# Paged sample attention: keys by gathered four-page tiles and 32x32 transposes on VectorE, side projections moved beside the keys

## The reference, cut to what matters

```python
def dsa_sample(q, k, v, iq, iw, ik, cache_k, cache_v, cache_idx_k, page_table, rel_bias):
    ...
    idx, valid = dsa_select(iq, iw, ik_all, q_pos, topk)      # best 256 of 2056 keys per query
    k_sel = jnp.where(is_past, cache_k[phys, slot].astype(k.dtype), gather(k, nidx))
    v_sel = jnp.where(is_past, cache_v[phys, slot].astype(v.dtype), gather(v, nidx))
    return dsa_attend(q, k_sel, v_sel, idx, valid, q_pos, rel_bias)

def dsa_attend(q, k_sel, v_sel, idx, valid, q_pos, rel_bias):
    logits = jnp.einsum('bthd,btkhd->bthk', q, k_sel).astype(jnp.float32) * ATT_SCALE
    logits = logits + bias                                    # T5 relative bias
    p = jax.nn.softmax(jnp.where(valid, logits, -jnp.inf), axis=-1)
    return jnp.einsum('bthk,btkhd->bthd', p, v_sel)
```

## Time and profile before

| | us |
|---|---|
| Median of three runs | 1596.6 |
| Span of the profiled execution | 1593.2 |
| Key stretch, group 0 / group 1 | 115.7 / 104.6 |
| Softmax stretch, group 0 / group 1 | 15.4 / 17.3 |
| Value stretch, group 0 / group 1 | 110.8 / 101.3 |

### The profile page before, as it was taken

How to read it: one execution, slowest core, us unless ns; L and a number is a source line. 1 busy time by engine, 2 the same in 40 slices (tenths; PEclk the granted TensorE clock), 3 DMA queues, 4 the chain that set the end, 5 groups by cost and what they waited for, 6 DMA issues and landing times.

```text
span 1593.2 us, 32571 instructions
## 1 busy us (share of the span) xinstructions
PE 1471.7 (92%) x13518; PEld 1334.5 (84%) x13518; DVE 762.0 (48%) x1030; ACT 511.5 (32%) x818; POOL 234.5 (15%) x371
## 2 busy tenths in 40 slices
PE   7999998979979989899998998899799999999995
PEld 4867798957867778797777998799699999999995
DVE  5288699496514540025540135543555555552123
ACT  4243223324323341023341122122344455442121
POOL 3423234154210000000000000321000110000000
PEclk8899999989999999999999999899799999999998
DMA  5415223122159979999869976133322233223221
GB/s 173 149 27 159 65 80 113 57 96 73 49 188 369 332 249 342 383 358 329 310 223 402 363 258 240 34 125 104 113 80 80 80 90 95 83 98 102 79 83 60
DMA packets 179278, 266.58 MB, mean 167 GB/s; under 512 B 20522, under 2 KB 136539, under 8 KB 178043
## 3 DMA queue, kind: packets, MB, share of 16 engines
q1 hardware_dynamic: 167947, 243.95, 44.5%
q0 software_dynamic: 5104, 11.11, 2.1%
q10 hardware_dynamic: 6080, 9.44, 1.6%
HBM read 240.28 MB, written 24.18 MB: 166 GB/s over the span
## 4 chain that ended last, share of the span: by engine, by line
PE 77%; DVE 8%; DMA 5%; ACT 3%; SPq 2%; issue 2%; POOL 2%; ACTq 0%; DVEq 0%
PE PS L987 14%; PE PS L989 13%; PE PS L988 13%; PE PS L1197 8%; PE PS L1210 4%; PE PS L1245 3%; PE PS L1319 3%; PE PS L1318 3%; PE PS L1317 3%; DMA R<-in_cache_v 3%; PE PS L1028 2%; PE PS L1029 2%; PE PS L1030 2%; PE PS L1173 1%; PE PS L1120 1%
## 5 line engine op out<-in xcount | busy, mean ns | idle before, releaser
L987 PE MATMUL PS<-xn_hi,WH 128*128 128x288 f32 (+1 forms) x1424 | 430.7, 302 | 16.0 <-DVE xn_lo L1614 13.2
L988 PE MATMUL PS<-xn_lo,WH 128*128 128x288 f32 (+1 forms) x1424 | 424.7, 298 | 0.0
L989 PE MATMUL PS<-xn_hi,WL 128*128 128x288 f32 (+1 forms) x1424 | 424.6, 298 | 0.0
L987 PEld LDWEIGHTS PS<-xn_hi,WH 128*128 128x128 f32 (+1 forms) x1424 | 271.1, 190 | 33.1 <-issue 22.2
L988 PEld LDWEIGHTS PS<-xn_lo,WH 128*128 128x128 f32 (+1 forms) x1424 | 271.9, 191 | 0.0
L989 PEld LDWEIGHTS PS<-xn_hi,WL 128*128 128x128 f32 (+1 forms) x1424 | 271.6, 191 | 0.0
L582 DVE TENSOR_TENSOR WL<-W,WH 128x2048 fp32r<-128x2048 f32 (+2 forms) x69 | 145.7, 2112 | 241.6 <-ACT WH L1358 241.6
L1358 ACT ACTIVATE WH<-W 128x2048 fp32r<-128x2048 f32 (+2 forms) x81 | 145.1, 1791 | 90.2 <-PE PS L1319 74.9
L1197 PE MATMUL PS<-CST,R 128*128 128x128 f32 x1024 | 142.7, 283 | 9.8 <-DMA R<-in_cache_k 9.5
L1793 DVE COPY RB<-PS 128x512 f32<-128x512 f32 x128 | 88.3, 691 | 115.7 <-PE PS L1197 115.7
L1197 PEld LDWEIGHTS PS<-CST,R 128*128 128x128 f32 x1024 | 112.1, 143 | 35.9 <-issue 25.7
(11 more groups left out here) (257 smaller groups left out, 2423.2 us busy)
## 6 DMA issues: line engine op xcount, KB each, us to landing
R<-in_cache_k SPq DMA_DIRECT2D x128, 512.0 KB, 5.3
R<-in_cache_v SPq DMA_DIRECT2D x128, 512.0 KB, 7.0
W<-in_w_in SPq DMA_DIRECT2D x30, 1024.0 KB, 5.4
W<-in_w_up SPq DMA_DIRECT2D x44, 512.0 KB, 4.6
W<-in_w_down SPq DMA_DIRECT2D x16, 704.0 KB, 4.4
x_scratch<-xT SPq DMA_DIRECT2D x2, 2304.0 KB, 9.0
W<-in_w_branch_a SPq DMA_DIRECT2D x4, 1024.0 KB, 7.9
W<-in_w_branch_b SPq DMA_DIRECT2D x4, 1024.0 KB, 6.1
```

Source lines behind the costliest of these rows:

```text
L987: pe.matmul(out, hi[:, k, cols], x.hi_block(n)[:, tokens], start=first, stop=False)
L988: pe.matmul(out, hi[:, k, cols], x.lo_block(n)[:, tokens], start=False, stop=False)
L989: return pe.matmul(out, lo[:, k, cols], x.hi_block(n)[:, tokens], start=False, stop=last)
```

## The change

1. Keys no longer come by page. POOL issues one indirect DMA per four-page tile (2 MB, `load_keys`), two tiles deep. Partition 32b+l gets the four consecutive keys 4l to 4l+3 of sequence b's page as one 16 KB row. The row numbers (32 x page + l) are computed once by POOL near the start from a copy of the page table (`PROW`, `KROW`, constant `lane`).
2. PE no longer transposes keys. DVE transposes each tile in two halves of 2048 columns, in 32x32 blocks, into three buffers (`KTB`). The queries are laid out for that (`QB`, 32 small ACT copies in place of POOL's), and each matmul contracts 32 dimensions of four sequences at once. A logit column now is 32r+l for key 4l+r, so `logits` reads the mask and writes its result with a step of four (`by_rest`).
3. The mask is written to and fetched from scratch by ACT instead of SP.
4. The side tiles leave the value stretches: two ahead of the first key stretch, eight and nine in the key stretches (`SIDE_K`), two in each softmax stretch, one at the end. Logit and output tiles now use single PSUM banks.

```diff
+    SIDE_K = [[1, 3, 5, 7, 9, 11, 13, 14], [0, 2, 4, 6, 8, 10, 12, 13, 14]]
-    put_side(('start',), 3)
+    put_side(('start',), 2)
     for G in range(2):
-        put_side(('softmax', G, 0), 1)
+        for kp in SIDE_K[G]:
+            put_side(('K', G, kp), 1)
+        put_side(('softmax', G, 0), 2)
         put_side(('softmax', G, 1), 0)
-        for b in range(4):
-            for kp, n in SIDE_V[4 * G + b].items():
-                put_side(('V', G, b, kp), n)
...
+        KR = [blocks(R1[:, 4096 * i:4096 * i + 4096], 4) for i in range(2)]
+        KTB = [blocks(a, 4) for a in (RB[:, 0:2048], R3[:, 0:2048], R3[:, 2048:4096])]
...
# page_freed: what a load waits for
+            if kind == 0 and n >= 8:
+                e.wait_ge(S_("k_transposed"), 32 * G + 2 * (n // 4 - 1))
+            elif kind == 0:
+                e.wait_ge(S_("v_pages_used"), 64 * G - 4 + 4 * (n // 4))
+            elif n < 8:
+                e.wait_ge(S_("k_transposed"), 32 * G + 30 + 2 * (n // 4))
             else:
-                e.wait_ge(S_("v_pages_used"), 64 * G + n + 1)
+                e.wait_ge(S_("v_pages_used"), 64 * G + n - 7)
...
+        def load_keys(e, G, kp):
+            page_freed(e, 128 * G + 4 * kp)
+            e.indirect_dma_start(out=R1[:, 4096 * (kp % 2):4096 * (kp % 2) + 4096], out_offset=None,
+                                 in_=cache_k[0].rearrange("n (k r) h d -> (n k) (r h d)", r=4),
+                                 in_offset=bass.IndirectOffsetOnAxis(ap=KROW[:, 16 * G + kp:16 * G + kp + 1], axis=0))\
+                .then_inc(key_in[kp % 2], 16)
...
# POOL
+            pool.memset(QB, 0.0).then_inc(S_("queries_cleared"), 1)
+            load_keys(pool, 0, 0)
             link(pool.memset(kTn[:, :, TS:P], 0.0))
             link(pool.tensor_copy(kTn[:, :, 0:TS], kT[:, :, TP:T]))
             link(pool.tensor_copy(QN, qT[:, :, TP:T]))
             pool.memset(ST[0:1, 110:111], 0.0).then_inc(S_("ring_free"), 1)
-            link(pool.memset(QZ, 0.0))
-            ...
+            load_keys(pool, 0, 1)
...
# PE, key stretch
-                for n in range(65):
-                    ...
-                                last = pe.transpose(bank('kp', G, n, u)[:, P * i:P * i + P],
-                                                    ring[seq % 8][:, HD * h:HD * h + HD], ident)
+                for kp in range(NPAGES):
+                    ...
+                    for u in range(2):
+                        pe.wait_ge(S_("k_transposed"), 32 * G + 2 * kp + u + 1)
+                        keys = KTB[(2 * kp + u) % 3]
+                        for j in range(4):
+                            for c in range(4):
+                                last = pe.matmul(bank('kl', G, kp)[32 * c:32 * c + 32, P * u:P * u + P],
+                                                 QB[:, G, 4 * u + c, j, :],
+                                                 keys[:, :, P * c + 32 * j:P * c + 32 * j + 32],
+                                                 start=(j == 0), stop=(j == 3))
+                    sides('K', G, kp)
...
# ACT: no key copies
-                    act.activation(KTb[n % 2][:, 0:4, :], blocks(bank('kp', G, n, 0), 4), ACT.Copy)\
-                        .then_inc(drains('kp', G, n, 0), 1)
+            for G in range(2):
+                for bb in range(4):
+                    for j in range(4):
+                        t = TP + 32 * G + 8 * bb
+                        last = act.activation(QB[32 * bb:32 * bb + 32, G, :, j, 8 * bb:8 * bb + 8],
+                                              qT[32 * j:32 * j + 32, :, t:t + 8], ACT.Copy)
...
# DVE
+                def transposed(kp):
+                    dve.wait_ge(key_in[kp % 2], 16 * (8 * G + kp // 2 + 1))
+                    for u in range(2):
+                        n = 2 * kp + u
+                        ...
+                        dve.transpose(KTB[n % 3], KR[kp % 2][:, :, 512 * u:512 * u + 512])\
+                            .then_inc(S_("k_transposed"), 1)
+
+                for kp in range(NPAGES):
+                    transposed(kp)
+                    if kp >= 2:
+                        logits(kp - 2)
```

More of the change, by code:

```diff
@@ L104, in shape_constants @@
     put('bucket', hot)
+    put('lane', np.tile((i % 32)[:, None], (1, 8)))
     return c
@@ L915, in _ @@
                 pool.memset(NBd[g][:, 192:256], 0.0).then_inc(S_("new_bias"), 1)
+            for kp in range(2, NPAGES):
+                load_keys(pool, 0, kp)
             drained(pool, 'kl', 0, NPG - 1)
```

163 lines of the change are left out of this document (83 added, 80 removed).

## The result

The changed kernel takes 1573.62 us (median of four runs, 1571.6 to 1582.9); the kernel before, run beside it, 1595.36. The two medians lie 21.7 us apart (1.4%). The ratio on record is not their quotient (0.9864) but 0.9892, with a 95% interval of 0.9861 to 0.9924: by it the change is faster by 1.1%, or 17 us. The forecast was 1555 us, a gain of 41.6 us, so about half of it came, or a little less. The sign was right and the size was not.

The account below looks back on a forecast made before the run. PE was taken to bound the key stretches, DMA the value stretches. Terms -8.5 + 5 - 36.5 + 16.4 + 5 - 27.0, plus 4 for the clock, gave -41.6 and a forecast of 1555 us, range 1523 to 1612.

Parts of the forecast that it names:

- cold clock: Behind the second value stretch: PE, idle before, restarts near 1.2 GHz, so 4 us added for the tiles there.
- load term: Key loop: 2.10 MB at 420 GB/s plus landing, 7.0 us; issue and hops 0.9; side traffic 1.0.
- the fill: Start of a key stretch: second tile 5.0 us after the first landed, then one tile every 7.1 us.
- eight pages waiting: Value stretch: eight pages already loaded, the other 56 at 1.25 us each; 74.3 us with 3.3 and 1.0 added.
- The loop is 14.2 us and P is 7.1 us: Key stretch: load, two transposes, buffer free, next load take 14.2 us; two buffers give period P per four-page tile.
- DVE not being free: Key loop: logits and chunk splits take DVE 1.3 us per tile, about half delaying a transpose, 0.7 us.
- starving buffer: Rival, 0.14: key loads under the double buffer land in 10 to 12 us, not 7.0; time 1603 to 1624.
- A landing time of 10 us or more: Sign for key loads that would make the prediction wrong; 10.0 us corresponds to a period of 8.6 us.
- PE at half clock in the key stretches: Rival, 0.04: PE stays at 1.2 GHz and bounds the key stretches at 8.85 us per tile; time 1604.
- DVE the bound: Rival, 0.06: key transposes take 4.61 us per half, so DVE needs 10.5 us per tile; time 1650.
- the fast end: Rival, 0.12: key transposes take 1.22 us per half and DMA's floor of 6.0 us rules; time 1524.
- POOL held off while DVE transposes: Rival, 0.04: a key load waits up to 2.3 us for a transpose, period 8.25 us; time 1587.

Follow-up runs that it names:

- e4: Changed kernel with each key load bringing only half its bytes (1 MB), transposes and all else kept; not a candidate version: 1537.5 us.
- e1: Changed kernel with four 1 MB key buffers in place of two of 2 MB, and 64 narrow matmuls per key tile in place of 32: 1585.1 us.
- e7: Changed kernel with the mask written before PE's last prompt tile and fetched as soon as the query copies are made: 1571.1 us.
- e2: Changed kernel with the side tiles put back where they stood before the change, so the new key path alone: 1604.8 us.
- e14: Changed kernel with each group's mask fetched by one DMA to 128 partitions in place of four to 32 partitions: 1602.0 us.
- e16: Changed kernel with each mask fetch shared between two queues, partitions 0 to 63 on one and 64 to 127 on another: 1577.5 us.
- e5: e1 with each side tile of the key stretches cut into four quarters of 12 matmuls: 1582.1 us.
- e10: Changed kernel with 1 MB key buffers, quarter side tiles, early mask, DVE's splits one key tile later, early maximum and last side tile moved back: 1565.7 us.
- e11: e10 with whole side tiles in place of quarters: 1591.3 us.

## Why the prediction was right in sign and wrong in size

By stretch, forecast and measured, in us:

| | forecast | measured | miss |
|---|---|---|---|
| keys 0 end at | 572 | 582.4 | +10.4 |
| softmax 0 | 20.4 | 19.2 | -1.2 |
| values 0 | 74.3 | 82.9 | +8.6 |
| keys 1 | 121 | 124.6 | +3.6 |
| softmax 1 | 22.3 | 19.1 | -3.2 |
| values 1 | 74.3 | 80.5 | +6.2 |
| cold clock behind it | 4 | 0 | -4 |

They add up to 20.4, and 1551.6 + 20.4 is 1572.0; the span is 1572.1.

Two steps failed. In the key stretches the loop's load term (7.0 + 0.9 + 1.0 us forecast, 10.2 measured) cost 12 us more than forecast and the fill (12.1 us forecast to the third tile, 18.8 and 15.2 measured) 10; shorter tails and an earlier first tile in group 1, less a start 1 us late in group 0, gave 8 of them back, which leaves 14.0. In the value stretches the 74.3 us (eight pages waiting, 1.25 us per page, 3.3 us for the next to land) were 82.9 and 80.5, 14.8 us more. Softmax and clock were forecast too dear; that they took back 8.4 us of these 28.8 is luck, not insight.

1. *The loop.* "The loop is 14.2 us and P is 7.1 us": measured 7.58 and 7.65. The mechanism was right; e4 moved it as it should, and e1 removed its wait. Its load term was too small: load, issue, hops and side traffic were set at 7.0 + 0.9 + 1.0 = 8.9 us and took 10.2, and 0.27 more for the hop from the second transpose to the issue. The 5.0 us in it were bytes over the full rate, as if the other buffer's load were not in flight; in the trace it is. The two transposes (2.27 and 2.31 us) were right. DVE not being free was set at 0.7 and, by 15.2 for the loop less 10.2, 0.27 and 4.6, is about 0.1. That is 0.5 us per tile, 6 us per stretch. It lies between the main case and the starving buffer, whose mechanism is what the trace shows. The prediction's own sign, "A landing time of 10 us or more", is met by 10.2 us from the issue, yet the pace did not reach that rival's 8.6: the rival put issue and side traffic (1.9 us) on top of a landing which, so measured, already holds them.
2. *The fill.* "5.0 to the second, 14 x 7.1": the third tile can start no sooner than one whole loop behind the first, 14.2 us, and I counted 12.1. That was an error in counting the loop, 2 us in each stretch. It took 15.2 us in group 1. In group 0 it took 18.8, with the mask's store and fetch in the way. e7 shows 2.3 us of that; the rest of it stays unassigned.
3. *Tails* were 2 to 3 us shorter than counted, and in group 1 the first tile landed 2.9 us behind the value stretch, not 6, because its load starts at page 60 and shares the DMA with the last pages instead of queueing behind them; that is a part of the next point.
4. *Value stretches.* "1.25 us" per page at 420 GB/s: over 60 us the rate is 408, 1.285 us, 2 us per stretch. The "eight pages waiting" helped little. In group 0 the softmax stretch is itself full (share 1.01 at 315 GB/s); five pages had landed when PE began at 601.6, the eighth was used at 605.85 and the ninth at 610.18, 8.6 us into the stretch and not 3.3. The whole stretch takes as long as 64 x 1.285 = 82.2 us. In group 1 the pages are there, but the DMA stands still until a place is free, and the ninth page is used 4.6 us into the stretch, the eleventh at 9.3:

```profile
828.20:830.20 2.00, 2.00 (x76) 2.00 (x80) 0.00 (x0) 0.00 (x0) 0.00 (x0) 1.00 0.04 8
840.00:900.00 60.00, 43.82 (x790) 25.95 (x790) 1.83 (x6) 0.92 (x6) 0.00 (x0) 0.69 1.03 408
```

   That side tiles were what slowed them is shown: e2 against the change. That the full softmax stretch costs group 0's pages their lead is read from the trace only; e14 and e16 changed the mask fetch that runs in it, but neither made it faster by more than 8%, and so did not settle it.
5. *Softmax and the cold clock.* A side tile in softmax was charged with 5 us of its 6.35 and the clock with 4 us. The stretches grew by 3.8 and 1.8 us only; PE idled 4.3 and 3.8 us in them before and 1.7 now. Behind the last stretch 663.4 us remain against 663.5, and the granted clock there reads 1.00 at once (908.7 to 915 us), though it was 0.72 over the value stretch: nothing of the 4 us came.
6. *PE at half clock in the key stretches*, *DVE the bound* and *the fast end* did not happen: clock 0.88 and 0.91, transposes at 2.3 us. Nor did *POOL held off while DVE transposes*: issues that overlap a transpose take 0.94 to 1.02 us, but for one, and that one began in a split (last section).

Behind it all stands one thing that I did not see: removing any one wait of the key stretch exposes the next (loaded keys, transposed keys behind a side tile, a split behind ACT, at last the side tiles' own bytes). The paces of e1, e5 and e10, 7.7 to 7.8, 7.2 to 7.6 and 6.6 to 7.0 us, show how close they stand. I had priced PE at 4.4 us per tile and taken it for free. An engine that is idle for nearly 40% of the tile by that price still holds others up if its work comes in pieces of 6.35 us and only three buffers stand before it (e11 against e10). In the changed kernel itself DVE did not wait for PE between 466 and 575 us; there the loop came first.

## What to carry to other kernels

A loop of two large buffers costs (landing + use) / 2 per buffer; take the landing time under two loads in flight, not bytes over rate, and count one whole loop for the fill. Halving the buffers helps only if every consumer behind them also works in small pieces: cut long side work into parts no longer than the slack of the smallest buffer, and let no in-order list carry an unrelated wait in front of the loop's next step. Where a side task disturbs a stream of loads, price its bytes as well as its engine time: in e10's first key stretch they alone explain the pace. And when an edit halves a tile, look at what it does to the number of instructions.
